# A two-block transformer in one kernel: the last shifted copies inside the convolution of the seventh chunk, its sums regrouped, and pair work ahead of weight halves in the attention heads

## What is computed

```python
def conformer_conv(h, w_pw1, b_pw1, w_dw, b_dw, ln_g, ln_b, w_pw2, b_pw2):
    u = h @ w_pw1 + b_pw1
    a, gate = jnp.split(u, 2, axis=-1)
    u = a * jax.nn.sigmoid(gate)
    u = jnp.pad(u, ((0, 0), (CONV_WIDTH - 1, 0), (0, 0)))          # 31 taps
    u = lax.conv_general_dilated(u, w_dw[:, None, :], ...) + b_dw   # depthwise
    u = jax.nn.silu(layer_norm(u, ln_g, ln_b))
    return u @ w_pw2 + b_pw2
...
# second model, even layer
fox_out = fox_attention(fq, fk, fv, log_f)                # 8 heads with forget gates
dsa_out = dsa_attention(q_lat, q_rope, c_kv, k_rope, iq, ik, iw, topk)   # 8 heads, keys by top 64
x = x + concat(fox_out, dsa_out) @ w_out_even
x = x + conv_glu_ffn(rmsnorm(x, g), w_up, conv_w, conv_b, w_down)
# second model, odd layer
x = x + moba_attention(rope(mq), rope(mk), mv) @ w_out_odd
x = x + conv_glu_ffn(...)
```

## Time and profile before

| | us |
|---|---|
| median of 3 runs | 1166.9 |
| lowest and highest | 1166.52 and 1168.44 |
| the profiled execution, its own time | 1168.28 |
| its span, from the first to the last instruction | 1166.4 |
| PE busy in it | 1143.9 |
| DVE busy | 828.7 |
| ACT busy | 657.9 |
| mean granted clock of PE | 0.995 |

### The profile page before, as it was taken

How to read it: one execution, slowest core, us unless ns; L and a number is a source line. 1 busy time by engine, 2 the same in 40 slices (tenths; PEclk the granted TensorE clock), 3 DMA queues, 4 the chain that set the end, 5 groups by cost and what they waited for, 6 DMA issues and landing times.

```text
span 1166.4 us, 26682 instructions
## 1 busy us (share of the span) xinstructions
PE 1143.9 (98%) x10651; PEld 974.7 (84%) x10651; DVE 828.7 (71%) x1320; ACT 657.9 (56%) x1019; POOL 131.6 (11%) x168
## 2 busy tenths in 40 slices
PE   9999999999999999999999999999999999999998
PEld 7778888888778888888877688888887778888887
DVE  6786777655786886655569759777666666987664
ACT  7664675433667476433475657564456656765432
POOL 0000200000203200000243220000124531000010
PEclk9999999999999999999999999999999999999999
DMA  8661375555362465555453337654575343755451
GB/s 338 259 206 53 103 245 208 178 187 211 113 249 96 136 240 190 206 182 185 152 203 109 110 109 254 211 175 149 181 256 181 110 165 107 262 192 190 149 178 56
DMA packets 31468, 206.59 MB, mean 177 GB/s; under 512 B 3488, under 2 KB 3872, under 8 KB 10144
## 3 DMA queue, kind: packets, MB, share of 16 engines
q1 hardware_dynamic: 31104, 205.00, 51.3%
q10 hardware_dynamic: 288, 0.52, 0.1%
HBM read 204.46 MB, written 1.05 MB: 176 GB/s over the span
## 4 chain that ended last, share of the span: by engine, by line
PE 89%; DVE 7%; ACT 2%; issue 1%; POOL 0%; DVEq 0%
PE ps L617 20%; PE ps L618 20%; PE ps L619 20%; PE ps L970 2%; DVE w_lo L2233 2%; PE ps L741 1%; PE ps L1397 1%; PE ps L880 1%; PE ps L648 1%; PE ps L1399 1%; PE ps L1398 1%; PE ps L726 1%; PE ps L882 1%; PE ps L881 1%; PE ps L643 1%
## 5 line engine op out<-in xcount | busy, mean ns | idle before, releaser
L1480 ACT ACTIVATE w_hi<-staged 128x2048 f16<-128x2048 f32 (+2 forms) x195 | 344.8, 1784 | 237.8 <-PE ps L619 229.2
L617 PE MATMUL ps<-f_hi,w_hi 128*128 128x256 f16 x1596 | 435.0, 273 | 0.2 <-issue 0.2
L618 PE MATMUL ps<-f_lo,w_hi 128*128 128x256 f16 x1596 | 435.0, 273 | 0.0
L619 PE MATMUL ps<-f_hi,w_lo 128*128 128x256 f16 x1596 | 435.0, 273 | 0.0
L2233 DVE SCALAR_TENSOR_TENSOR w_lo<-staged,w_hi 128x2048 f16<-128x2048 f32 (+2 forms) x195 | 415.0, 2142 | 24.2 <-ACT w_hi L1480 24.0
L617 PE MATMUL ps<-x_hi,w_hi 128*128 128x256 f16 x696 | 189.8, 273 | 0.6 <-DVE tmp L2586 0.6
L618 PE MATMUL ps<-x_lo,w_hi 128*128 128x256 f16 x696 | 189.7, 273 | 0.0
L619 PE MATMUL ps<-x_hi,w_lo 128*128 128x256 f16 x696 | 189.7, 273 | 0.0
L618 PEld LDWEIGHTS ps<-f_lo,w_hi 128*128 128x128 f16 x1596 | 156.2, 98 | 19.3
L617 PEld LDWEIGHTS ps<-f_hi,w_hi 128*128 128x128 f16 x1596 | 156.2, 98 | 18.6 <-issue 0.4
L619 PEld LDWEIGHTS ps<-f_hi,w_lo 128*128 128x128 f16 x1596 | 156.2, 98 | 18.0
(11 more groups left out here) (375 smaller groups left out, 1790.9 us busy)
## 6 DMA issues: line engine op xcount, KB each, us to landing
staged<-weights SPq DMA_DIRECT2D x165, 1024.0 KB, 5.2
staged<-weights SPq DMA_DIRECT2D x32, 704.0 KB, 4.3
xn<-bands SPq DMA_DIRECT2D x3, 512.0 KB, 9.9
m<-bands SPq DMA_DIRECT2D x3, 512.0 KB, 8.0
cst<-constants SPq DMA_DIRECT2D x1, 1027.0 KB, 7.9
h<-x_turned SPq DMA_DIRECT2D x2, 512.0 KB, 4.6
staged<-weights SPq DMA_DIRECT2D x2, 512.0 KB, 6.9
qT<-bands SPq DMA_DIRECT2D x2, 512.0 KB, 11.5
```

The lines of the kernel that those rows point to most:

```text
L617: pe.matmul(out, wh, xh[:, c, :], start=(c == 0), stop=False)
L618: pe.matmul(out, wh, xl[:, c, :], start=False, stop=False)
L619: last = pe.matmul(out, wl, xh[:, c, :], start=False, stop=(c == kc - 1))
L1480: act.activation(w_hi[:, s, o:o + n], staged[:, s, o:o + n], ACT.Copy, scale=SW).then_inc(hi_split, 1)
```

## The change

In the convolution `copy_rows(7)` moves from behind `convolve(6)` to its middle, and `convolve` gets a first and a last step for that. `sum_bands` runs over chunks 0 to 3 and then 4 to 6. The one-column products L1001 move into the middle of `convolve(7)`. Of the `fill` products behind the first `rows_of`, 10 become 3 and 24 become 21. ACT's load of the square root's table moves behind `convolved(6)`, DVE's last `split` behind `shift(7)`, and DVE's reciprocal ahead of `centre(0)`.

In the even layer ACT rounds half 11 two steps later, DVE makes `sel` behind `rope_query(0)` and half 11 behind `add_rope_keys(0)`, `rope_query(3)` moves ahead of half 14, and on PE `swap_query(3)` and parts of `behind_pairs` move forward. In the odd layer `score_pair(7)` comes one chunk of `behind_pairs` earlier, and DVE makes half 14 behind `rope_pair(7)`.

```diff
-            def ended_pairs(kind, p):
+            def ended_pairs(kind, p, third=0):
...
-                behind_pairs(kind, (2,), 0, 6)
+                behind_pairs(kind, (2,), third, 6)
...
                 gate_or_value(2 * j + 1)
-                convolve(j - 1)
+                if j < DC - 1:
+                    convolve(j - 1)
+            convolve(DC - 2, 0, TAP_STEPS // 2)
             copy_rows(DC - 1)
+            convolve(DC - 2, TAP_STEPS // 2)
             sum_bands(range(0, 4))
-            sum_bands(range(4, 6))
-            sum_bands(range(6, 7)).then_inc(group_summed, 1)
-            convolve(DC - 1)
+            sum_bands(range(4, 7)).then_inc(group_summed, 1)
+            convolve(DC - 1, 0, TAP_STEPS // 2)
             pe.wait_ge(group_taken, 2)
...
+            convolve(DC - 1, TAP_STEPS // 2)
             fill(5, 2)
...
-            fill(10, 2)
+            fill(3, 2)
             pe.wait_ge(ln_step, 3)
             rows_of(8, 7).then_inc(ln_rows, 1)
-            fill(24, 4)
+            fill(21, 4)
...
             turn_pair("even", 5)
-            behind_pairs("even", (0,), 3, 4)
-            out_pair("even", 5)
-
             pe.wait_ge(drained["even"], 21)
             swap_query(3)
-            behind_pairs("even", (1,), 0, 4)
+            behind_pairs("even", (0,), 3, 4)
+            behind_pairs("even", (1,), 0, 2)
+            out_pair("even", 5)
+
+            behind_pairs("even", (1,), 2, 4)
             behind_pairs("even", (0, 1), 4, 5)
             score_pair("even", 7)
+            behind_pairs("even", (0, 1), 5, 6)
+            arrived(2 * FIRST["oute"] + 1)
+            behind_pairs("even", (2,), 0, 3)
             turn_pair("even", 6)
-            behind_pairs("even", (0, 1), 5, 6)
+            behind_pairs("even", (2,), 3, 6)
             out_pair("even", 6)
-            ended_pairs("even", 7)
+            ended_pairs("even", 7, 6)
...
-            behind_pairs("moba", (0, 1), 3, 5)
+            behind_pairs("moba", (0, 1), 3, 4)
             score_pair("moba", last_pair)
             turn_pair("moba", last_pair - 1)
-            behind_pairs("moba", (0, 1), 5, 6)
+            behind_pairs("moba", (0, 1), 4, 6)
...
-            act.activation(by_token[:, 0:1], by_token[:, 11:12], ACT.Sqrt)
             shift(DC - 1)
             convolved(DC - 2)
+            act.activation(by_token[:, 0:1], by_token[:, 11:12], ACT.Sqrt)
...
             exp_pair("even", 2)
-            even_split(11, 11)
             fox_rows(14, 3, 1)
             high_pair("even", 1)
+            even_split(11, 11)
...
-                for g in LOW_SPLITS[j][-1:]:
-                    split(g)
+                if j < DC - 1:
+                    for g in LOW_SPLITS[j][-1:]:
+                        split(g)
             shift(DC - 1)
+            split(LOW_SPLITS[DC - 1][-1])
...
+            dve.wait_ge(group_taken, 3)
+            dve.reciprocal(by_token[:, 8:10], by_token[:, 6:8]).then_inc(ln_step, 1)
             dve.wait_ge(ln_rows, 1)
             centre(0)
-            dve.wait_ge(group_taken, 3)
-            dve.reciprocal(by_token[:, 8:10], by_token[:, 6:8]).then_inc(ln_step, 1)
...
             low_pair("even", 1)
-            chain(dve.tensor_scalar(sel[:], idx[:, TOPK // 8 % 2, :], TAKEN / 2, MASKED, ALU.is_gt, ALU.mult))
-            chain(dve.tensor_tensor(sel[:], sel[:], k("causal"), ALU.add))
-
-            even_split(11)
+
             reduce_pair("even", 3)
             add_rope_keys(0)
+            even_split(11)
             invert_pair("even", 3)
             low_pair("even", 2)
             rope_query(0)
+            chain(dve.tensor_scalar(sel[:], idx[:, TOPK // 8 % 2, :], TAKEN / 2, MASKED, ALU.is_gt, ALU.mult))
+            chain(dve.tensor_tensor(sel[:], sel[:], k("causal"), ALU.add))
...
             reduce_pair("even", 6)
+            rope_query(3)
             even_split(14)
             low_pair("even", 5)
             invert_pair("even", 6)
-            rope_query(3)
...
-            for g in ODD_SPLITS[last_pair - 1][1:]:
-                split(2 * u0 + g)
+            split(2 * u0 + 13)
             invert_pair("moba", last_pair - 1)
             low_pair("moba", last_pair - 2)
             rope_pair(last_pair)
+            split(2 * u0 + 14)
             reduce_pair("moba", last_pair)
```

More of the change, by code:

```diff
@@ L959, in copy_rows, with convolve @@
                     last.then_inc(copies, 1)
-            def convolve(j):
-                pe.wait_ge(band_lo, j + 1)
-                pe.wait_ge(shift_lo, 2 * j + 2)
-                if j:
-                    pe.wait_ge(conv_drained, 2 * j - 1)
-                for step in range(TAP_STEPS):
+            def convolve(j, first=0, end=TAP_STEPS):
+                if first == 0:
+                    pe.wait_ge(band_lo, j + 1)
+                    pe.wait_ge(shift_lo, 2 * j + 2)
+                    if j:
+                        pe.wait_ge(conv_drained, 2 * j - 1)
+                for step in range(first, end):
                     for e, (w, x) in enumerate(((0, 0), (0, 1), (1, 0))):
@@ L972, in convolve @@
                                              start=(step == 0 and e == 0), stop=(step == TAP_STEPS - 1 and e == 2))
-                last.then_inc(conv_product, 1)
+                if end == TAP_STEPS:
+                    last.then_inc(conv_product, 1)
             def sum_bands(chunks):
```

## The result

The kernel after takes 1159.64 us, the median of 5 runs from 1159.21 to 1160.21. The kernel before, with two more runs beside it, stands at 1166.9 (5 runs, 1164.91 to 1169.88). The ratio of after to before is 0.9936, with a 95% interval of 0.9921 to 0.9951. The forecast was 1161.8, the range 1158.8 to 1165.0: right in sign, in the range, 2.2 us too high.

A forecast was written before the change was run, and what follows sets the result against it. PE, busy 98% of the span, was taken as the bound, so gains come mainly from its stalls: 0 + 2.6 + 1.65 + 0.8 + 0.7 = 5.75 off 1168.28 gives 1162.5, less 0.7 for the median: 1161.8 us, range 1158.8 to 1165.0.

The forecast's parts named there:

- The wait of the sums: Convolution, ahead of its first sum: PE is out of instructions, not held by ACT; the 2.0 us wait shrinks to 1.75.
- rival 1: Convolution: the sums' wait belongs to ACT or instructions come in time, sums start at 84.6, 1159.1 us; chance 0.14.
- so I keep the 1.65 for it: Convolution: the low clock behind the sums' wait, costing 1.65 us, was taken to stay after the change.
- sister of rival 1: Convolution: instructions stay late, but the shorter wait leaves the clock up, 1160.9 us; no chance of its own given.
- -0.35 + 0.35 = 0: Convolution: 0.35 us lost as PE waits for the squares, 0.35 won by DVE's earlier reciprocal; bounds 0.4 either way.
- chunk 6 is long squared: Convolution: as PE resumes late, the regrouped sums have no wait for chunk 6 left to hide; gain nothing.
- Even layer, first half: Moving ACT's rounding and DVE's mask and half frees the score and swap: 2.9 - 0.3 = 2.6 us, plus 1.65 of clock.
- Even layer, second half: Earlier swap_query(3) and 15 products ahead of pair 6's turn fill waits of 0.8 and 0.4, 0.4 left: gain 0.8 us.
- Odd layer: One half leaves rope_pair(7)'s way and six products cover the 0.3 behind the turn; gain 0.7, wait of 0.9 to 1.0 stays.
- rival 2: Even layer: the wait moves to the next step, pair 4 and later pairs wait, costing 1 to 2.5 us, about 1164.8; chance 0.15.
- rival 3: PE's instruction packets fall elsewhere; each new stall costs 3.65 us, one gives 1166.1, two 1169.8, slower than before; chance 0.06.
- rival 4: Heads: the change doesn't do what it says, since another engine holds the same step; 1166.9 us; chance 0.05.

## Why the prediction was right, and where it was off

**The wait of the sums is one for instructions: right, and shown.** I forecast a wait of 1.6 to 1.9 us with a packet at 84.0, and PE going on at about 86.5; it was 1.80, 83.9 and 86.33. Idle products wait there as well, and moving the block boundary removes it. The Trainium skill ("Runtime: NRT & Kernel Launch", Instruction fetch mechanics) says that crossing a block is mostly hidden. Here three crossings were not, at 0.55 to 1.37 us around 46 us, 1.7 to 2.0 at 84 and 0.31 to 0.94 at 91, over the profiles that have them. Weights filled the transfer engines ahead of each packet: in before their share is 1.03 from 38 to 44.5 us, which the rows ahead of the prediction don't show, and 0.87 from 77 to 84.

**The range held partly by luck.** The measured 1159.64 lies outside the forecast's own band of 1160.5 to 1163.3. It is in the range because that was drawn down for rival 1, at 1159.1. Rival 1 is refuted as it was put: the sums still start at 86.33 and not before 85. The time came near it by another way.

**The step that failed: "so I keep the 1.65 for it".** I took the low clock behind the sums as certain because both waits of 2.0 us in one profile had it. The clock stayed at 1.00, as it did in ten of the eleven profiles that have this wait, and by their mean clocks in all 30 runs of the kernels with this convolution and this wait. That is what the sister of rival 1 said, at 1160.9. Whether the shorter wait kept the clock up, as the sister has it, is not shown. One execution can't tell a rule from an accident. The same holds for the swap, where the fall is common (four profiles in five) but not certain.

**The term "-0.35 + 0.35 = 0" of the convolution: nearly right.** The old convolution at full clock stands in the kernel with the even layer's part alone; the last part of its sums, and that of the kernel after:

```profile
93.14 0.58 PE L1007 MATMUL ps<-cst,sq 128*128 128x1 f32 x4
```

```profile
93.03 0.59 PE L1012 MATMUL ps<-cst,sq 128*128 128x1 f32 x4
```

From the first sum to here takes 7.31 us in the one, 6.37 without its second wait for instructions of 0.94, and 6.70 in the other: 0.33 lost, where I had 0.35. From here to L648 it takes 6.42 and 5.93: 0.49 won, where I had 0.35. So the 1.77 us of the convolution are the 1.65 of clock, which I had counted as staying, and 0.1 to 0.2 of edits.

What I had not seen is what stands behind a clock that stays up. Against the old convolution at full clock (13.73 and 13.46 us from the first sum to L648) the new one takes 12.63, which is 0.8 to 1.1 less, and 0.66 to 0.94 of that is the second wait for instructions, which the new one doesn't have. I priced DVE's moved half at nothing ("one transfer of weights starts 2.3 us later"). In the kernel after the transfer was what would have held the packet; with the half moved back, this stretch takes 0.58 more. And "chunk 6 is long squared" holds only while PE is late; once it isn't, ACT's edit brings 0.69 in the trace.

**Even layer, first half: 2.6 forecast, 2.4 measured** (the 5.41 of the even layer, less the 1.67 of clock and the 1.34 of the second half). The swap waits for nothing, as forecast; the score of pair 4 waits 0.40 where I took 0.2 to 0.3.

**Even layer, second half: 0.8 forecast, 1.34 measured.** The mis-sized step is "so 0.4 is left" at the turn of pair 6. In the trace of after that turn starts at 667.03 and the view shows no wait for it. The 15 products that now stand ahead of it cover POOL although `invert_pair(6)` is later.

**Odd layer: 0.7 forecast, 0.64 measured,** with the wait of 0.86 that I had put at 0.9 to 1.0.

**Rivals 2 to 4.** The next step of the even layer did wait, but 0.4, far from the 1 to 2.5 of rival 2. No new late packet came (rival 3). The parts work alone (rival 4 falls).

By these terms the forecast of 1162.5 for the profiled execution misses 1160.21 by 2.3: convolution 1.8, even layer 0.4, start 0.3, less 0.1 in the odd layer. The 0.7 that I took off for the median came out at 0.57 between this profile and its median, which is luck: I took it off for a low stretch that would be there in some runs only, and by their mean clocks (0.998 to 1.0) no run of the kernel after has one.

## What to carry to other kernels

Where PE stops in front of an instruction whose inputs have long been ready, look at the instruction queue: a packet that starts 2.2 to 2.6 us ahead of PE's resumption, at the end of a burst of weights, was the releaser each time here, whatever name the view gave. Such a wait was not cured by reordering the engines that feed PE, but by moving the block boundary (here 116 small idle products at the start) or the transfer ahead of the packet (here one weight half made later). And before a low-clock stretch goes into a sum, see it in more than one execution, also in the mean clock of runs without a profile, and ask what it hides.

## What the hardware did that I had not expected

- A block boundary can be moved on purpose. 176 more PE instructions at the start, at the same start of the real work, took 2.8 us out of the convolution of the kernel after and 1.9 to 2.3 out of its median time; its three waits for instructions (0.32, 0.55 and 1.80, of which the last had been named ACT's) went at once, and none over 0.25 us appeared elsewhere.
- A clock at 0.50 seems to have hidden a wait. By my reading the stretch cost 1.65 us of PE's work and saved 0.66 to 0.94 of waiting for the next packet; net it made the old convolution only 0.7 to 0.9 us longer (14.40 against 13.73 and 13.46).
- After the same wait of 1.97 us at the same place the clock fell in four profiles and stayed up in a fifth, and by their mean clocks 68 of 111 runs of such kernels have a low stretch. With idle products in the wait none of 12 has.
- One and the same DVE step on the mask (the sum with `causal`, 128x384) took 0.56 us when it stood ahead of the keys and 0.85 in the kernel after. The traces point at POOL: in the kernel after POOL is at work from 643.3 to 646.5 us, over both steps of the mask (0.55 and 0.85); with the mask first it is idle, and they take 0.35 and 0.56; in before it works until 641.2, over most of the first step and none of the second, and they take 0.71 and 0.56. No run was made to try it.
